# Two experts side by side in the second expert layer, and a rearranged join between the two blocks

## The reference, cut to what matters

```python
hid = silu(xg @ w_gate[e]) * (xg @ w_up[e]);  y = (hid @ w_down[e]) * router_weight
x   = x + gate_row * (sum over experts of y, added back at each expert's tokens)
x   = x * rsqrt(mean(x * x) + eps) * final_norm_g            # the final norm of block 1
h   = x * rsqrt(mean(x * x) + eps) * norm1_g_2 ...           # the first norm of block 2
```

## Time and profile before

| | us |
|---|---|
| median of 3 runs (lowest, highest) | 2527.1 (2525.88, 2529.19) |
| the profiled execution's own time | 2523.93 |
| its span, first to last instruction | 2522.0 |
| PE busy in it | 2035.4 (81%) |
| first expert layer, first up matmul to last addition | 654.6 to 1595.0 |
| from there to block 2's first projection | 1595.0 to 1618.4 |
| second expert layer, first up matmul to last addition | 1988.7 to 2507.1 |

### The profile page before, as it was taken

One profiled execution on the slowest core, in us unless ns is written; L12 is line 12 of the kernel. 1 busy time (PEld: TensorE's weight loads), 2 busy tenths in 40 slices (PEclk: granted clock), 3 DMA queues, 4 the chain that ended last, 5 costly groups with the idle time before them and its releaser, 6 DMA issues.

```text
span 2522.0 us, 30967 instructions
## 1 busy us (share of the span) xinstructions
PE 2035.4 (81%) x12214; PEld 1196.4 (47%) x12214; DVE 588.6 (23%) x1151; ACT 378.0 (15%) x728; POOL 109.5 (4%) x107
## 2 busy tenths in 40 slices
PE   4999979786666676777766666599998699999996
PEld 2676767575222232222222222388787444444443
DVE  2324446433100000000000000332522322222223
ACT  2022222100000000000000100121520111111111
POOL 0002211200000000000000000000200000000000
PEclk8999889767776767677776767699999799999998
DMA  7223323314799999999999999334344799999993
GB/s 299 84 88 146 134 101 134 125 51 187 289 422 422 422 422 422 422 422 422 422 422 422 422 422 422 148 134 138 118 150 156 312 386 395 386 389 393 388 394 133
DMA packets 102582, 729.26 MB, mean 289 GB/s; under 512 B 11409, under 2 KB 11889, under 8 KB 15985
## 3 DMA queue, kind: packets, MB, share of 16 engines
q1 hardware_dynamic: 98928, 714.94, 70.2%
q10 hardware_dynamic: 3584, 13.35, 1.4%
HBM read 727.15 MB, written 1.10 MB: 289 GB/s over the span
## 4 chain that ended last, share of the span: by engine, by line
PE 67%; DMA 19%; DVE 6%; issue 3%; ACT 3%; POOL 1%; DVEq 0%; ACTq 0%; POOLq 0%; SPq 0%
DMA ring<-in_w_down 17%; PE psum L696 9%; PE psum L480 7%; PE psum L824 6%; PE psum L724 5%; PE psum L468 4%; PE psum L1124 3%; PE psum L704 3%; PE psum L507 3%; PE psum L674 2%; PE psum L1041 2%; PE psum L1305 2%; PE psum L1326 2%; PE psum L1115 2%; PE psum L1056 1%
## 5 line engine op out<-in xcount | busy, mean ns | idle before, releaser
L480 PE MATMUL psum<-ring,main 128*32 128x512 f32 x2048 | 278.6, 691 | 91.3 <-ACT main L551 35.0
L499 PE MATMUL psum<-ring,main 128*32 128x512 f32 x1024 | 175.3, 808 | 82.8 <-DMA ring<-in_w_down 70.3
L696 PE MATMUL psum<-ring,main 128*64 128x256 f32 x2048 | 226.5, 379 | 0.7 <-ACT main L782 0.7
L480 PEld LDWEIGHTS psum<-ring,main 128*32 128x32 f32 x2048 | 63.7, 122 | 288.1 <-issue 177.9
L696 PEld LDWEIGHTS psum<-ring,main 128*64 128x64 f32 x2048 | 147.1, 137 | 87.9 <-issue 17.7
L824 PE MATMUL psum<-main,ring 128*128 128x256 f32 x768 | 169.5, 380 | 0.0
L824 PEld LDWEIGHTS psum<-main,ring 128*128 128x128 f32 x768 | 146.2, 191 | 21.8 <-issue 0.5
L468 PE MATMUL psum<-main 128*128 128x32 f32 x512 | 112.6, 402 | 33.7 <-DVE main L532 33.7
L468 PEld LDWEIGHTS psum<-main 128*128 128x128 f32 x512 | 110.4, 332 | 56.7 <-DVE main L532 56.7
L539 DVE TENSOR_TENSOR main<-main,psum 128x512 f32<-128x512 f32 x16 | 11.0, 687 | 532.4 <-ACT main L554 532.4
L499 PEld LDWEIGHTS psum<-ring,main 128*32 128x32 f32 x1024 | 31.3, 135 | 209.5 <-DMA ring<-in_w_down 141.3
(11 more groups left out here) (389 smaller groups left out, 2351.1 us busy)
## 6 DMA issues: line engine op xcount, KB each, us to landing
ring<-in_moe_w SPq DMA_DIRECT2D x192, 1024.0 KB, 8.9
ring<-in_w_gate SPq DMA_DIRECT2D x128, 1024.0 KB, 26.1
ring<-in_w_up SPq DMA_DIRECT2D x128, 1024.0 KB, 25.9
ring<-in_w_down SPq DMA_DIRECT2D x128, 1024.0 KB, 21.0
ring<-in_w_mod SPq DMA_DIRECT2D x48, 1024.0 KB, 6.8
ring<-in_w_in SPq DMA_DIRECT2D x36, 1024.0 KB, 4.8
ring<-in_w_out SPq DMA_DIRECT2D x8, 1024.0 KB, 4.9
ring<-in_w_rnn_out SPq DMA_DIRECT2D x8, 640.0 KB, 3.8
```

The lines of the kernel that those rows point to most:

```text
L480: last = mm(psum[32 * j:32 * j + 32, b, :], xg1[:, k, :], slot(n % SLOTS)[:, 512 * j:512 * j + 512], start=k == 0, stop=k == KT - 1)
L499: last = mm(psum[q:q + 32, BANK_Y, :], hidT[:, P * (f % 4) + 32 * (f // 4):P * (f % 4) + 32 * (f // 4) + 32], w[:, r, 512 * g:512 * g + 51 ...
L696: last = nc.tensor.matmul(psum[64 * q:64 * q + 64, b, 0:256], xg2[:, k, c // 2, :], w[:, k, 256 * q:256 * q + 256], start=c < 2 and k == 0 ...
```

## The change

Three things.

1. **Second expert layer.** The unit is now a pair of experts, whose 64 places each stand side by side as 128 columns. `gather2` multiplies each 128 by 128 tile of the tokens with the pair's 0/1 matrix (16 full-array matmuls of 128 columns), which gives the gathered tokens already turned; `turn_tokens2` and ScalarE's copy ahead of it are gone, and the router weights are turned by 2 transposes. `up2` is called in two halves of 16 matmuls of 512 columns, in which the two experts' matmuls stand side by side (form 128\*64), each with its own weights. The hidden rows of both are one 128 by 512 tile: 4 transposes. `down2` has 16 matmuls of 512 columns for the pair. `spread_out2` is 2 full-array matmuls of 512 columns for each 128 tokens, once for a pair, between and behind the two halves of `up2`; its result and `down2`'s share two PSUM banks. The chunks of the two experts alternate in the ring, and SyncE's loop runs once for a pair with 12 chunks, as before.
2. **First expert layer.** VectorE moves y out of PSUM and multiplies with the gate row (`gate_y`, two loads of 64 by 512 in place of one of 128 by 1024) and adds the spread result straight to `x`. The clearing of `acc` and the multiplication and addition behind the layer are gone.
3. **Between the blocks.** ScalarE takes the sums of squares of x and of x times the gain; GpSimd works out both norms' factors from them, separately for each 128 tokens; VectorE writes block 2's normed tokens first and `x` after. TensorE turns the first 128 tokens as soon as they are there; copies out of PSUM are shared by VectorE and ScalarE. The constant table is loaded when the layer is done, TensorE no longer waits for it, and SyncE no longer waits for `block1_ready`.

```diff
...
+gate_y = take(512)
...
     V.tensor_tensor(hid, sgate, psum[:, BANK_U, :], ALU.mult).then_inc(m_hid, 1)
+    dve.wait_ge(m_chunk_used, 24 * e + 24)
+    dve.wait_ge(m_spread, 2 * e + 1)
+    V.tensor_tensor(ysb, psum[:, BANK_Y, :], gate_y, ALU.mult).then_inc(m_y, 1)
     for t in range(NT):
         dve.wait_ge(m_spread, 2 * e + t + 2)
         dve.wait_ge(m_acc, 2 * e + t + 1)
...
+        V.tensor_tensor(x[:, t, :], x[:, t, :], psum[:, BANK_S:BANK_S + 2, :].rearrange("p b n -> p (b n)"),
                         ALU.add).then_inc(m_acc, 1)
...
-    act.activation(ysb, psum[:, BANK_Y, :], ACT.Copy).then_inc(m_y, 1)
...
+BANK_XG, BANK_G2, BANK_U2, BANK_T2, BANK_P2, BANK_Y2 = 0, 2, 3, 4, 5, 6
+def moe2_load(sp, i, n):
+    u, c = n % 2, n // 2
+    name, h = (("moe_w1", 0), ("moe_w3", 0), ("moe_w1", 1), ("moe_w3", 1), ("moe_w2", 0), ("moe_w2", 1))[c]
...
 def gather2(pe, i):
...
+    for k in range(KT):
+        for t in range(NT):
+            last = nc.tensor.matmul(psum[:, BANK_XG + k // 4, P * (k % 4):P * (k % 4) + P], u2[:, t, P * k:P * k + P],
+                                    onehot2[:, t, :], start=t == 0, stop=t == NT - 1)
...
+    pe.wait_ge(n_spread_sb, i + 1)
+    for t in range(NT):
+        last = nc.tensor.transpose(psum[:, BANK_P2, P * t:P * t + P], gated2[:, t, :], ident)
...
+def up2(pe, i, j, h):
+    if h == 0:
...
+    for m, b in enumerate((BANK_G2, BANK_U2)):
+        n = 4 * h + 2 * m
...
+        for u in range(2):
...
         for k in range(4):
...
+            for u in range(2):
+                last = nc.tensor.matmul(psum[CAP2 * u:CAP2 * u + CAP2, b, :], xg2[:, 4 * h + k, CAP2 * u:CAP2 * u + CAP2],
+                                        w[u][:, k, :], start=h == 0 and k == 0, stop=h == 1 and k == 3)
+                if k == 3:
...
 def spread_out2(pe, i, u, t):
...
+    pe.wait_ge(n_spread_sb, i + 2)
...
     for g in range(2):
...
+        last = nc.tensor.matmul(psum[:, BANK_Y2 + g, :], spread2[:, u, P * t:P * t + P], y2[:, 512 * g:512 * g + 512],
+                                start=True, stop=True)
...
 def turn2(pe, i):
...
+    for c in range(4):
+        last = nc.tensor.transpose(psum[:, BANK_T2, P * c:P * c + P], hid2[:, P * c:P * c + P], ident)
...
+def down2(pe, i, j):
...
+    pe.wait_ge(n_acc, 2 * i + 1)
     for q in range(2):
...
+        n = 8 + 2 * q
...
+        for u in range(2):
...
         for c in range(2):
             for g in range(2):
...
+                for u in range(2):
+                    f = P * (2 * q + c) + CAP2 * u
+                    last = nc.tensor.matmul(psum[CAP2 * u:CAP2 * u + CAP2, BANK_Y2 + g, :], hidT2[:, f:f + CAP2],
+                                            w[u][:, c, 512 * g:512 * g + 512], start=q == 0 and c == 0, stop=q == 1 and c == 1)
+                    if c == 1 and g == 1:
...
+def two_pairs_tensor(pe, j, first=False, final=False):
     for u in range(2):
...
+        up2(pe, i, i, 0)
         if not (first and u == 0):
             spread_out2(pe, i - 1, 1 - u, 0)
+        up2(pe, i, i, 1)
+        if not (first and u == 0):
+            spread_out2(pe, i - 1, 1 - u, 1)
         turn2(pe, i)
...
             gather2(pe, i + 1)
...
+        down2(pe, i, i)
 def onehot_2(dve, i, e):
...
+    dve.wait_ge(n_gates, i + 1)
+    for t in range(NT):
+        for u in range(2):
...
+            nc.vector.tensor_scalar(onehot2[:, t, CAP2 * u:CAP2 * u + CAP2], K("slot"), pos, None, ALU.is_equal)
+            last = nc.vector.tensor_scalar(gated2[:, t, CAP2 * u:CAP2 * u + CAP2], K("slot"), pos, gate, ALU.is_equal, ALU.mult)
...
 def hidden2(dve, i):
...
+    nc.vector.tensor_tensor(hid2, sg2, psum[:, BANK_U2, :], ALU.mult).then_inc(n_hid, 1)
+def add2(dve, i, t):
+    dve.wait_ge(n_spread, 2 * i + t + 2)
...
+    nc.vector.tensor_tensor(acc2[:, t, :], acc2[:, t, :], psum[:, BANK_Y2:BANK_Y2 + 2, :].rearrange("p b n -> p (b n)"),
+                            ALU.add).then_inc(n_acc, 1)
+def two_pairs_vector(dve, p, jj, first=False, final=False):
     for u in range(2):
...
+        i, e = PAIRS2 * p + 2 * jj + u, 4 * jj + 2 * u
...
+            onehot_2(dve, i + 1, e + 2)
+        if not (first and u == 0):
+            add2(dve, i - 1, 0)
         hidden2(dve, i)
         if not (first and u == 0):
...
+            add2(dve, i - 1, 1)
+def read_gathered2(act, i, u):
...
+    nc.scalar.activation(xg2.rearrange("p k s -> p (k s)"), psum[:, BANK_XG:BANK_XG + 2, :].rearrange("p b n -> p (b n)"),
+                         ACT.Copy).then_inc(n_xg, 1)
+    act.wait_ge(n_gates, i + 2)
+    nc.scalar.activation(spread2[:, u, :], psum[:, BANK_P2, 0:S], ACT.Copy).then_inc(n_spread_sb, 1)
+def two_pairs_scalar(act, j, first=False, final=False):
     for u in range(2):
...
+        act.wait_ge(n_chunk_used, 12 * i + 8)
...
+        nc.scalar.activation(sg2, psum[:, BANK_G2, :], ACT.Silu).then_inc(n_silu, 1)
...
+        nc.scalar.activation(hidT2, psum[:, BANK_T2, :], ACT.Copy).then_inc(n_hidT, 1)
...
+            read_gathered2(act, i + 1, 1 - u)
+        act.wait_ge(n_chunk_used, 12 * i + 12)
+        act.wait_ge(n_spread, 2 * i + 1)
+        nc.scalar.activation(y2, psum[:, BANK_Y2:BANK_Y2 + 2, :].rearrange("p b n -> p (b n)"), ACT.Copy).then_inc(n_y, 1)
...
 def block2_tensor(pe, flip):
...
     pe.wait_ge(m_acc, 2 * E1 + 1)
-    pe.wait_ge(const2_loaded, 16)
     for kk in range(4):
...
+        banks.new(("uT", kk))
...
-        pe.wait_ge(xn2_ready, NT)
...
+    for t in range(NT):
+        pe.wait_ge(xn2_ready, t + 1)
+        for kk in range(4):
+            o = banks.tile(("uT", kk))
+            for c in range(2):
                 last = flip(o[:, S * c + P * t:S * c + P * t + P], xn2[:, t, P * (2 * kk + c):P * (2 * kk + c) + P])
...
+            if t == NT - 1:
+                last.then_inc(banks.when_full(("uT", kk)), 1)
     for kk in range(4):
...
     gather2(pe, 0)
...
             sp.wait_ge(m_chunk_used, 24 * E1 - SLOTS + s + 1)
...
-                sp.wait_ge(block1_ready, 1)
...
-    for i in (1, 2, 3):
+    for i in (1, 2):
         load_row(0, rows, i, rows_loaded[0])
+    for g in range(2):
+        act.dma_start(gate_y[64 * g:64 * g + 64, :],
+                      mod_rows[0:1, D * ROW_OF[3] + 512 * g:D * ROW_OF[3] + 512 * g + 512].to_broadcast([64, 512])).then_inc(rows_loaded[0], 16)
...
+    act.wait_ge(m_acc, 2 * E1 + 1)
+    act.dma_start(c2, A["const2"]).then_inc(const2_loaded, 16)
+    for t in range(NT):
+        act.activation(acc[:, t, :], x[:, t, :], ACT.Square, accum_out=rstat[:, 10 + t:11 + t]).then_inc(act_step, 1)
...
-    act.wait_ge(block1_ready, 1)
-    act.dma_start(c2, A["const2"]).then_inc(const2_loaded, 16)
...
+        act.wait_ge(xg_ready, t + 1)
+        act.activation(acc[:, t, :], h2[:, t, :], ACT.Square, accum_out=rstat[:, 14 + t:15 + t]).then_inc(act_step, 1)
...
+        act.sem_inc(squares_ready, 1)
+    for kk in (1, 3):
+        act.wait_ge(*banks.full(("uT", kk)))
+        o = banks.tile(("uT", kk))
+        for c in range(2):
+            k = 2 * kk + c
+            act.activation(uT[:, k, :], o[:, S * c:S * c + S], ACT.Identity, scale=scale2[:, k:k + 1], bias=mfm[:, 1, 0, k:k + 1]).then_inc(act_step, 1)
...
-    V.memset(acc, 0.0).then_inc(dve_step, 1)
...
-        V.tensor_tensor(acc[:, t, :], acc[:, t, :], rows[:, 3, :], ALU.mult).then_inc(dve_step, 1)
...
-        V.tensor_tensor(x[:, t, :], x[:, t, :], acc[:, t, :], ALU.add).then_inc(dve_step, 1)
...
-    dve.sem_inc(block1_ready, 1)
+    dve.wait_ge(m_acc, 2 * E1 + 1)
     V.scalar_tensor_tensor(scale2, mfm[:, 1, 0, KT:2 * KT], 1.0, M("norm1_2"), ALU.add, ALU.mult).then_inc(dve_step, 1)
...
+    for t in range(NT):
+        V.tensor_tensor(h2[:, t, :], x[:, t, :], rows[:, 1, :], ALU.mult).then_inc(xg_ready, 1)
+    for t in range(NT):
+        dve.wait_ge(rstd_ready, 3 + t)
+        dve.wait_ge(xg_ready, 1 + t)
+        V.tensor_scalar(xn2[:, t, :], h2[:, t, :], rstat[:, 20 + t:21 + t], None, ALU.mult).then_inc(xn2_ready, 1)
+    for t in range(NT):
+        V.tensor_scalar(x[:, t, :], h2[:, t, :], rstat[:, 12 + t:13 + t], None, ALU.mult).then_inc(dve_step, 1)
...
+    for kk in range(0, 4, 2):
...
+    for t in range(NT):
+        pool.wait_ge(squares_ready, 3 + t)
+        rsqrt(rstat[:, 12 + t:13 + t], rstat[:, 10 + t:11 + t], 1, 1.0 / D, EPS)
+        V.tensor_scalar(rstat[:, 16 + t:17 + t], rstat[:, 14 + t:15 + t], rstat[:, 12 + t:13 + t], rstat[:, 12 + t:13 + t],
+                        ALU.mult, ALU.mult).then_inc(pool_step, 1)
...
+        rsqrt(rstat[:, 18 + t:19 + t], rstat[:, 16 + t:17 + t], 1, 1.0 / D, EPS)
+        V.tensor_tensor(rstat[:, 20 + t:21 + t], rstat[:, 18 + t:19 + t], rstat[:, 12 + t:13 + t], ALU.mult).then_inc(pool_step, 1)
...
+        pool.sem_inc(rstd_ready, 1)
...
```

More of the change, by code:

```diff
@@ L671, in gather2 @@
             pe.wait_ge(n_xg, i + 1)
-            for t in range(NT):
-                for g in range(2):
```

(36 more changed lines are left out.)

212 lines of the change are left out of this document (71 added, 141 removed).

## The result

The median after is 2463.8 us (2461.51 to 2465.39, 4 runs), against 2527.01 before (2525.88 to 2529.19, 4 runs on the same chip): a ratio of 0.9748 [0.9731, 0.9765]. The profiled executions took 2465.39 and 2523.93, their spans 2463.4 and 2522.0, so 58.6 us went. The medians lie 63.2 apart: the profiled execution before was quicker than all four that give its median, the one after was the slowest of its four. The table divides the 58.6; the other 4.6 us it can't place.

The account below looks back on a forecast made before the run. The second layer was taken as bound by TensorE's phases, the first by DMA. Terms -46.2 (layer), +1.0 (its start), -9.7 (between blocks), +0.1 and +0.4 (first layer) sum to -54.4: forecast 2470 us, range 2461 to 2488.

Parts of the forecast that it names:

- turn and router weights: Second layer, per pair: 4 transposes once at 0.58 us; 2 transposes at 0.37 for 2 x 0.64.
- So the transfers fall back by 0.5 us a pair against 9 us in hand and TensorE never waits: Second layer: DMA needs 29.8 us a pair against TensorE's 29.3, hidden down to 414 GB/s.
- Rival A: Second layer: DMA becomes the bound; at 400 GB/s the last chunks come 15.6 us late, 2485 us; chance 0.12.
- Start of the layer: Second layer, one-hots to first up matmul: +1.0 us, between +0.3 (upper clock level) and +3.0 (lower).
- TensorE reached the upper level after its first 3 us before: Second layer's start: clock behaviour of the old kernel, given beside the choice of +1.0 us.
- Between the blocks: 13.8 for 13.7: Last addition to first projection: 13.7 us for 23.34, 9.7 less; bounds 8 and 11.
- Rival C: Between the blocks: ScalarE's copies or GpSimd's longer chain eat the gain, 2 us for 9.7; 2478 us; chance 0.06.
- held 6.4 us of waiting for the constants: Between the blocks: the old chain waited 6.4 us for constants behind SyncE's weights, which is gone.
- The 0.1 for y: First layer: VectorE's 0.69 us in place of ScalarE's 0.60 counts only behind the last chunk, +0.1.
- All of the gain comes through: Block 2's mixers are TensorE's own work, so the 9.7 us gained between the blocks stays.
- B: Second layer's gather: weight loads of 0.192 us don't hide, a pair costs 6.1 more; 2568 us; chance 0.04.
- D: Second layer: side-by-side matmuls of `up2` and `down2` stop overlapping, 20 us more a pair; 2790 us; chance 0.01.

Follow-up runs that it names:

- half-bytes kernel: Changed kernel with each chunk's DMA bringing only half its bytes from the second layer's second pair on; 2464.34 us, 0.9755, the layer 466.2 for 468.0.
- shortened spread: Changed kernel with each matmul that spreads y back covering 64 of 512 columns; 2463.95 us, 0.9741, the layer 464.6.
- kept_warm: Changed kernel with 61 spare matmuls in TensorE's waits and x written after block 2's tokens are copied; 2461.78 us against 2468.01 for the changed kernel.
- rest_alone: Kernel before with everything of the change but the second expert layer (parts 2 and 3); 2519.59 us, 0.9951.

## Why the prediction was right, and where it was not

**The direction and the mechanism.** The second layer was TensorE's own phases, and the pair's phases came out as priced: up 13.99 (14.0), spread 3.73 (3.8), turn 0.43 (0.6), gather 3.58 (3.6), router weights 0.31 (0.4), down 6.92 (6.9); 28.96 for 29.3. The mis-sized terms are the small ones, turn and router weights. They were taken from rows in which these transposes stand between phases of other forms; now the turn stands between two full-array phases and the router weights follow one, and between those a change of phase costs nothing that the rows show. Of the 0.34 us a pair they make 0.26; over 14 pairs the whole is 4.8 us. The first pair took 26.7 (27.1). The last with the tail took 34.9 (34.9), which is luck: 0.9 of it is waiting for chunks, which the prediction put at nothing, and with half the bytes it takes 34.0. So TensorE's own length was priced 6.0 us too long (472.2 for 466.2), and the 1.8 us of DMA made the error 4.2.

**"So the transfers fall back by 0.5 us a pair against 9 us in hand and TensorE never waits"** failed. With 28.96 a pair and 29.8 for its chunks they fall back by 0.86, 12 us over 14 pairs, and what is in hand is used up in the last two: distances of 29.07 and 29.80, then 0.65 in the last up. It cost 1.8 us (the half-bytes kernel). The landing times grew as foretold. Rival A put the floor too high (400 GB/s, where 422 was held), but its mechanism, DMA as the bound, begins right here, and the shortened spread shows it.

**Start of the layer: +2.1 for +1.0.** The step that failed is carrying over "TensorE reached the upper level after its first 3 us before": in the changed kernel the stretch of the first gather had 0.66 in the mean, and the gather took 6.1 us for 3.6. It is within the bounds given (+0.3 to +3.0), and `kept_warm` shows that it is the clock: with TensorE busy ahead of it the same gather takes 3.6 and the start 6.7.

**Between the blocks: 13.8 for 13.7.** The first half is as worked out (squares done at 2.9, normed tokens started at 5.5). The second starts at 8.6 instead of 8.0: GpSimd begins its second half at 5.6 instead of 5.3, and the first instruction there takes 0.69 us where it takes 0.19 in the first half, for a reason no row shows. Its transposes, at a granted clock of 0.50, end at 11.4 for 10.6. The copies, two engines side by side, make up for it (2.1 from the last transpose for 2.7), so the close 13.8 holds two errors that cancel. Rival C is refuted. What was wrong is the sentence on the old chain, that it "held 6.4 us of waiting for the constants": taking that wait away alone gives 1.0. The sum wasn't built on it, and so was not hurt.

**First layer.** ScalarE's four row loads put the first router's matmul at 581.53 for 581.00, 0.5 later as priced (0.4). The 0.1 for y can't be seen. **Mixers.** "All of the gain comes through" held in this pair of profiles (-0.2); `rest_alone` shows that it can be given back farther on, by the clock.

**The sum.** The forecast for the profiled execution was 2469.5, and it took 2465.39. The median, 2463.8, is 6 below the forecast of 2470: 4 of these come from the stages, the rest from the profiled execution being the slowest of its four.

**Rivals B and D** are refuted: 0.112 us a record of the gather against 0.19 for its load alone, and 32 side-by-side records of 512 columns in 6.97 us.

## What to carry to other kernels

Price a change of tiling by the distance between the starts of phases, and take short phases from rows with the same neighbours; what was priced so held to 0.1 us, and the two terms that had other neighbours did not. Before counting on a shorter phase, list what it hides: here the spread covered two hand-overs to other engines, and an eighth of its columns gave only a third of its worth. When two limits lie within a few per cent (28.96 against 29.8 a pair), the reserve in the ring decides how long the slower one stays hidden, so multiply the difference by the number of rounds.

## What the runs showed of the hardware

- A full-array float32 stream whose records each load 128 by 128 weights has a floor of 0.11 us a record at the upper level of the clock: 8, 64 and 128 moving columns take 3.5 to 3.6 us for 32.
- Between two streams of the full-array form a change of phase was not to be seen: 4 transposes and the 32 records of the gather behind them start 0.43 and 3.58 us before what follows, 0.11 a record.
- One core's queue held 422 GB/s from 2010 to 2400 us, beside a TensorE busy for 389.4 of the 390. It is the rate of the first layer too, where TensorE has time to spare, and with half the bytes the pairs stayed 28.96 apart: neither slowed the other.
- Matmuls that nobody reads, in waits of 3 to 13 us, raised the granted clock of the work behind them (0.65 to 0.84, 0.62 to 0.89) and, with x written later, gave 3.9 us by the stages.
- Block 2's mixers lasted 363.3 us at a mean granted clock of 0.94 in one profile and 369.8 at 0.92 in another, with the same 1542 records of TensorE.
